# Which weight chunks are multiplied unsplit in fp32 behind four normalizations

## The reference, cut to what matters

```python
h = rms_norm(x, g_pre_mix)                    # norm 0
proj = h @ w_in                               # 1024 x 2560
...                                           # attention, recurrence
x = x + rms_norm(mix, g_post_mix)
h = rms_norm(x, g_pre_ffn)                    # norm 1
up = causal_dwconv(h @ w_up, w_conv_ffn)      # 1024 x 5632
x = x + rms_norm(ffn, g_post_ffn)
...
h = _rmsnorm(x) * (1 + scale) + shift         # norm 2, then norm 3
qkv = h @ w_qkv                               # 1024 x 3072
gate, up = jnp.split(h @ w_gu, 2, axis=-1)    # 1024 x 5632
```

## Time and profile before

| | |
|---|---|
| median of 3 runs | 1262.53 us (1262.05 to 1265.84) |
| span of the profiled execution | 1258.0 us |
| own time of that execution | not listed beside its span; the median of the runs is 4.5 us over the span |
| TensorE busy | 1224.1 us, 97% |
| VectorE busy | 1016.2 us, 81% |
| ScalarE busy | 779.0 us, 62% |
| GpSimd busy | 93.1 us, 7% |

### The profile page before, as it was taken

The page is one execution under the profiler, slowest core; times in us unless marked ns, Lnnn a source line. Parts: engine busy times, 40 slices in busy tenths (PEclk is TensorE's granted clock), DMA queues, the critical chain, the costliest instruction groups (busy, mean ns, idle before and its releaser), DMA issues.

```text
span 1258.0 us, 20244 instructions
## 1 busy us (share of the span) xinstructions
PE 1224.1 (97%) x7668; PEld 1086.8 (86%) x7668; DVE 1016.2 (81%) x1095; ACT 779.0 (62%) x992; POOL 93.1 (7%) x111
## 2 busy tenths in 40 slices
PE   9989999999999999999999999999999999999995
PEld 7978999987998799998897777898989898989884
DVE  6797899996756588777756578989898989898987
ACT  5765666644655455443346556777777777777764
POOL 0020000000562100000002202000000000000020
PEclk9999999999999999999999999999999999999998
DMA  9953997679944569998973239999999999999991
GB/s 322 377 200 102 337 314 270 246 289 252 250 159 162 181 215 325 332 349 308 382 253 97 79 140 394 379 406 355 401 351 409 348 408 349 408 345 411 347 410 73
DMA packets 163981, 369.08 MB, mean 293 GB/s; under 512 B 24420, under 2 KB 96559, under 8 KB 157511
## 3 DMA queue, kind: packets, MB, share of 16 engines
q1 hardware_dynamic: 157345, 350.72, 78.0%
q10 hardware_dynamic: 5094, 12.11, 2.5%
q0 software_dynamic: 1472, 5.28, 1.1%
HBM read 360.72 MB, written 14.70 MB: 298 GB/s over the span
## 4 chain that ended last, share of the span: by engine, by line
PE 71%; DVE 12%; ACT 4%; issue 4%; DMA 3%; SPq 3%; POOL 2%; ACTq 0%; DVEq 0%
PE ps L1341 20%; PE ps L795 7%; PE ps L797 7%; PE ps L796 7%; PE ps L1368 6%; PE ps L807 4%; PE ps L809 4%; PE ps L811 4%; DVE wlo L1893 3%; SPq L712 2%; PE ps L859 2%; PE ps L867 2%; DMA raw<-in_moe_w_gu 2%; DVE third_lo L1893 2%; DVE wlo L1885 1%
## 5 line engine op out<-in xcount | busy, mean ns | idle before, releaser
L1406 ACT ACTIVATE whi<-raw 128x1024 fp32r<-128x1024 f32 x186 | 192.6, 1057 | 152.0 <-PE ps L797 96.1
L1885 DVE TENSOR_TENSOR wlo<-raw,whi 128x1024 fp32r<-128x1024 f32 x186 | 227.1, 1248 | 72.8 <-ACT whi L1406 69.3
L795 PE MATMUL ps<-ahi,whi 128*128 128x256 f32 x832 | 234.3, 282 | 0.3 <-ACT qT L1591 0.3
L796 PE MATMUL ps<-alo,whi 128*128 128x256 f32 x832 | 231.8, 279 | 0.0
L797 PE MATMUL ps<-ahi,wlo 128*128 128x256 f32 x832 | 231.8, 279 | 0.0
L1893 DVE TENSOR_TENSOR wlo<-raw,whi 128x1792 fp32r<-128x1792 f32 (+1 forms) x96 | 199.3, 2089 | 24.4 <-ACT whi L1420 24.3
L1420 ACT ACTIVATE whi<-raw 128x1792 fp32r<-128x1792 f32 (+1 forms) x96 | 167.5, 1758 | 55.9 <-PE ps L1368 24.0
L795 PEld LDWEIGHTS ps<-ahi,whi 128*128 128x128 f32 x832 | 156.9, 189 | 1.7 <-issue 0.8
L796 PEld LDWEIGHTS ps<-alo,whi 128*128 128x128 f32 x832 | 156.7, 188 | 0.7 <-issue 0.7
L797 PEld LDWEIGHTS ps<-ahi,wlo 128*128 128x128 f32 x832 | 156.9, 189 | 0.0
L1341 PE MATMUL ps<-whi,hchi 128*128 128x448 f32 x352 | 101.8, 370 | 4.0 <-DVE wlo L1893 2.7
(11 more groups left out here) (350 smaller groups left out, 2431.7 us busy)
## 6 DMA issues: line engine op xcount, KB each, us to landing
raw<-in_moe_w_gu SPq DMA_DIRECT2D x96, 896.0 KB, 7.0
ada<-in_w_ada SPq DMA_DIRECT2D x48, 1024.0 KB, 7.4
raw<-in_moe_w_down SPq DMA_DIRECT2D x32, 1024.0 KB, 7.9
ada<-in_moe_w_gu SPq DMA_DIRECT2D x32, 896.0 KB, 7.3
raw<-in_w_up SPq DMA_DIRECT2D x22, 1024.0 KB, 5.8
raw<-in_ffn_w_gu SPq DMA_DIRECT2D x22, 1024.0 KB, 9.1
ada<-in_moe_w_down SPq DMA_DIRECT2D x16, 1024.0 KB, 9.2
raw<-in_na_w_qkv SPq DMA_DIRECT2D x12, 1024.0 KB, 8.4
```

Of the source, the lines that this page charges most:

```text
L795: pe.matmul(o, h[:, k, cols], bhi[:, k], start=(k == 0), stop=False)
L796: pe.matmul(o, h[:, k, cols], blo[:, k], start=False, stop=False)
L1406: act.activation(high_, src, ACT.Copy).then_inc(hi_done, 1)
L1885: ve.tensor_tensor(low_, src, high_.bitcast(F32), ALU.subtract).then_inc(lo_done, 1)
```

## The change

Behind norms 0 to 3 only the first weight chunk stays unsplit. The second is split like all others, and its two ScalarE copies and two VectorE subtractions are put into the norm itself: ScalarE copies both halves right behind the last square root, before it modulates tile 1 (at norm 0, behind the activation copies). VectorE subtracts the first half before the four `alo`, the second half behind them (at norm 0, both behind them). TensorE's order at norms 1 to 3 becomes: turn tile 0; tile 0 of the first chunk, its first column tile and then its second; turn tile 1; tile 1 of the first chunk; the second chunk in split form. `gate_up` starts at its first step and leaves out its first chunk, and `projection` starts with chunk 1; the wait for the activations' pairs moves from the third chunk to the second. Since the second chunk now fills a split buffer, the fourth chunk's copies wait for it. `whole_pair` stays in use for the latent attention (norm 4), whose chunks are both unsplit as before.

```diff
+SECOND_CHUNK = {0: W_IN + 1, 1: W_UP + 1, 2: W_QKV + 1, 3: W_GU + 1}
-WHOLE = [c for first in (W_IN, W_UP, W_QKV, W_GU, W_MDN) for c in (first, first + 1)]
+WHOLE = [W_IN, W_UP, W_QKV, W_GU, W_MDN, W_MDN + 1]
...
-            def whole_columns(first, s, banks, after_turn=None):
-
-                pieces = two_tiles(banks)
-                w = whole_pair(first, s, (256, 256), pieces, after_turn)
-                for i in range(2):
-                    whole_rest(w[i], pieces[i], s)
+            def whole_columns(first, s, bank, after_turn=None):
+
+                fill(2, {1: 0, 3: 2}.get(s, 0))
+                turn(s, 0)
+                if after_turn:
+                    after_turn()
+                w = whole_raw(first, 256)
+                pieces = two_tiles((bank,))[0]
+                for piece in pieces:
+                    whole_side([(w, piece)], 0, s)
+                turn(s, 1)
+                whole_rest(w, pieces, s)
...
             def gate_up(gu, stage):
-                for j in range(1, GU_STEPS):
+                for j in range(GU_STEPS):
...
-                        columns_form(gu + 2 * j + part, [ps[:, 2 * (j % 2) + part, f * S:(f + 1) * S] for f in range(2)], ahi, alo,
-                                     AT0[stage] if (j, part) == (1, 0) else None)
+                        if (j, part) != (0, 0):
+                            columns_form(gu + 2 * j + part, [ps[:, 2 * (j % 2) + part, f * S:(f + 1) * S] for f in range(2)],
+                                         ahi, alo, AT0[stage] if (j, part) == (0, 1) else None)
...
-            for c in range(2):
-                if c:
-                    pe.wait_ge(sem("vecs_ready"), 1)
-                w = whole_raw(W_IN + c, 256)
-                for piece in first_pair[c]:
-                    whole_side([(w, piece)], 0, 0)
-                whole_rest(w, first_pair[c], 0)
+            w0 = whole_raw(W_IN, 256)
+            for piece in first_pair[0]:
+                whole_side([(w0, piece)], 0, 0)
+            whole_rest(w0, first_pair[0], 0)
+            pe.wait_ge(sem("vecs_ready"), 1)
+            columns_form(W_IN + 1, [o for o, _ in first_pair[1]], ahi, alo, AT0[0])
...
-            for c in range(2, 12):
-                pe.wait_ge(sem("qkv2_free"), c - 1)
+            for c in range(1, 12):
+                if c >= 2:
+                    pe.wait_ge(sem("qkv2_free"), c - 1)
...
+                if s in SECOND_CHUNK and s:
+                    split(SECOND_CHUNK[s])
                 modulate_tile(s, 1, scale, shift)
...
             norm_by_tile(0, vec("g_pre_mix"))
+            split(W_IN + 1)
...
+                if s:
+                    split(SECOND_CHUNK[s], (0,))
                 for n in range(KT // 2):
...
+                split(SECOND_CHUNK[s], (1,) if s else (0, 1))
```

More of the change, by code:

```diff
@@ L870, in whole_pair @@
             def whole_pair(first, s, widths, pieces, after_turn=None, before_turn=None):
-                fill(2, {1: 0, 3: 2}.get(s, 0))
                 turn(s, 0)
@@ L1080, in projection @@
             def projection(first, c, rows, b, free, stage, step):
-                turn0 = AT0[stage] if c == 2 else None
+                turn0 = AT0[stage] if (stage, c) == (2, 1) else None
                 if rows:
@@ L1126, in _ @@
             sum_columns(0, (0,), 3)
-            whole_columns(W_UP, 1, (0, 1), lambda: sum_columns(0, (1,), 3, KT))
+            whole_columns(W_UP, 1, 0, lambda: sum_columns(0, (1,), 3, KT))
             pe.wait_ge(sem("mod_read0"), 1)
@@ L1130, in _ @@
             output_projection(W_DOWN, FT, tiles(ghi), tiles(glo), 1, sem("gT_ready1"))
-            whole_columns(W_QKV, 2, (6, 7))
+            whole_columns(W_QKV, 2, 6)
             def step2(i):
@@ L1159, in _ @@
             output_projection(W_NAO, KT, *mixes[2], 2, begun=2, last=HEADS0[3] // 2)
-            whole_columns(W_GU, 3, (0, 1))
+            whole_columns(W_GU, 3, 0)
             gate_up(W_GU, 3)
```

## The result

Twelve executions of each kernel on the same chip: before 1261.20 us median, after 1266.39. The ratio is 1.0038, 95% interval 1.0025 to 1.0052, so the change costs 0.4%, some 4.8 us (the medians are 5.2 apart), just beyond the 0.3% that the prediction gave as what a measurement of this kernel can tell. One execution of the kernel before took 4995.69 us; it hardly moves the median. The forecast was no change, 1262.5 us in a range to 1266.2; the median lies just above that range, and the change made the kernel slower. The forecast's starting point, 1262.53 us from three executions, was itself 1.3 us above the median of the twelve.

The account below looks back on a forecast made before the run. The prediction took TensorE's order of work as the bound (busy 1224 of 1258 us). Its terms, -1.5 - 1.5 + 3.9 - 0.9, summed to 0.0 us, so 1262.5 us, range 1258.0 to 1266.2.

Parts of the forecast that it names:

- norm 0: Norm 0: chunk 1's halves come in time and the attention behind passes the saving on; -1.5 us, bounds 0 to -1.5.
- norm 1: Norm 1: the saving is kept, with under 0.1 us of modulation showing; 10.72 us becomes 9.23, so -1.5.
- norm 2, order and meeting: Norm 2: lost cover and VectorE meeting GpSimd's additions outweigh the saving; +3.9 us, bounds -1.2 and +3.9.
- norm 3: Norm 3: the order costs 0.2 us at the turn and 0.15 at the modulation; -0.9 us net, bounds -0.5 and -1.5.
- (a): Norm 2, tile 0: the whole second column tile follows the wait, so tile 1's turn and everything behind come 0.8 us later.
- (b): Norm 2: VectorE's subtractions alternate with GpSimd's bias additions, which start at 319.73 whatever TensorE does; 1.06 us lost each time.
- (c): Norm 2: TensorE waits for VectorE in the second chunk; the third chunk starts at 331.8 instead of 327.88, so +3.9 us.
- the bias for the second eight heads: Norm 2: its additions cost GpSimd another 11.01 us later, independently of TensorE, and could give back 0.3 us.
- the doubt in that step: Norm 0: unknown whether attention, paced by VectorE and queued transfers until 60 us, passes the gain on: 0 to -1.5 us.
- Rival D: Slower, by the clock: norm 2's waits bring low-clock stretches of 1.7 us; one gives 1264.2, two 1265.9, three 1267.6; chance 0.14.
- that place as safe: Norm 2, 309.5 to 313.3 us: TensorE busy 2.08 of 3.80 us, yet the clock kept 1.00.
- the common term: All four edits: an unsplit chunk takes 7.15 us, a split one 5.63; each saves 1.5 us of TensorE work, 6.1 in all.

Follow-up runs that it names:

- the changed kernel again: The changed kernel, unaltered, run a second time with a new profile: 1.0034 (1.0015 to 1.0052) of the kernel before.
- the pair without the additions: Changed kernel and kernel before, each without GpSimd's first eight mask additions at norm 2: 0.9955 and 1.0000 of the kernel before; medians 1258.74 and 1262.94 us.
- the later start: GpSimd's first eight mask additions at norm 2 wait for third-chunk splits: changed kernel 1.0004, kernel before 0.9986, norms 0 to 2 0.9992, norms 0 and 1 0.9983.
- the kernel before again: The kernel before, unaltered, run again with a new profile: 1.0000; the profiled execution took 1263.20 us.

## Why the prediction was wrong

From turn to turn, all profiles (20 in all; at norm 2 those with GpSimd's additions left out or moved are left out, and at norm 1 the one with small matmuls):

| term | forecast | measured | from |
|---|---|---|---|
| norm 0 | -1.5 | -0.5 | 107.5 (mean of 11) against 108.0 (9) |
| norm 1 | -1.5 | -1.11 | 190.33 to 190.37 against 191.44 to 191.48 |
| norm 2, order and meeting | +3.9 | +4.0 | 137.86 (one profile) against 133.9 (mean of 7), no low clock in any |
| norm 2, low clock in tile 0 and a fifth meeting | 0 | +0.8 | mean of 6 is 138.64, the one with dummy matmuls among them; +0.5 if the old order's one profile with a low clock is counted too (134.1, mean of 8) |
| norm 3 | -0.9 | -0.6 to -0.8 | 196.03 against 196.59, 191.55 against 192.32 |
| sum | 0.0 | +2.6 | |
| share of the long pitch behind norm 3 | not in it | +2.1, an estimate | norm 3 alone is +1.3 to +1.6, less its own -0.6; each of the two is uncertain by 2 |

The last two lines together are +4.7 us; the three comparisons of the changed kernel with the kernel before gave +4.8, +4.3 and +5.2. The same terms give +4.8 for norm 2 alone (measured +4.8), +3.2 for norms 0 to 2 (+3.2), -0.1 for norms 0, 1 and 3 (+0.1), -1.1 for norm 1 (-1.8) and -1.6 for norms 0 and 1 (+0.3, in the interval). These agreements bear out the sum and not each term: every measured value is uncertain by some 2 us.

**Norm 2** was right in mechanism and in size, by its three steps. (a) The turn of tile 1 comes 7.86 us behind that of tile 0, 6.97 before: 0.89 for 0.8. (b) 1.07 us a meeting for 1.06. The count was short: GpSimd did not start at 319.73 "whatever TensorE does" but at 316.69, 10.2 us behind the turn and not 11.2 (in the profiles with its additions in their place it started anywhere from 9.2 to 13.3 us behind), and all four activation subtractions met it. With the earliest start seen under the new order, 9.5 us in the changed kernel again, the first added subtraction met it too (2.1 us), the fifth meeting of the table. TensorE was 2.05 us earlier itself, so only 1 us of the 3 counted. (c) The third chunk came 24.6 us behind the turn in place of the forecast 23.3, and attention took some of it back, so that +4.0 meets +3.9 as closely as it does is in part luck. The Trainium skill ("SBUF — State Buffer", SBUF: two separate sides) says that GpSimd and a VectorE operation with two SBUF inputs take the shared ports by an exclusive lock, each for a whole instruction. The trace agrees: 0.63 us alone, 1.70 beside GpSimd, the same loss for every one. What I added at the end of that part, that the bias for the second eight heads could give something back, did not matter.

**Norm 1** lost 0.39 us of its 1.5 where I had said that under 0.1 would show: the matmuls of tile 1 start 1.04 us behind the turn's start in place of 0.87 and take 3.94 us, not 3.74, which I put down to the modulation that nothing covers now. **Norm 3** loses the same way: tile 1 takes 4.13 us for 3.74. **Norm 0** is a step that failed: I gave its bounds as 0 and -1.5 and took the full end. The raw saving came as forecast: from the first turn to the recurrence's gates, the first matmuls behind the projection, TensorE takes 29.03 us before and 27.53 in the one changed profile with the same pitch there. But by the turn of norm 1 only 0.5 of it is left in the mean. In the two first profiles the lead is still 2.2 us at the last scores before 65 us; then TensorE stands 2.41 us instead of 1.55 for the attention's `probs`, and the lead is 1.0 by 83 us. So the attention between took it back, as the doubt in that step said; which engine or transfer paces it was not tested. These three are 1.6 us of the miss.

**The clock.** Rival D had the right sign. At norm 2 the nine profiles with the new order have twelve low stretches of 3.4 us (one of 6.8 counted as two), the other eleven have one. But the price is by place. Behind the stops of the second chunk a stretch cost nothing in the first profile, since the third chunk waits for VectorE anyway (137.85 us with one, 137.86 without). In tile 0, at 311 us, it costs 1.1 to 1.5 (turn to turn of the tiles 8.9 to 9.4 us against 7.86; 10.07 with the one of 6.8 us). The Trainium skill ("TensorE: Matmul & The Clock Gate", HAM oscillation) describes the like, short bursts of matmuls with waits between them behind which the clock is low; the trace agrees here in six of nine profiles. I had read that place as safe because the clock kept 1.00 there in the earlier trace rows. With the new order the first gap there is as before (1.10 us), the burst behind it is shorter (8 matmuls in 1.44 us instead of 16 in 2.02) and the second gap longer (1.22 us instead of 0.64). The stretch at 64 to 66 us costs nothing that shows: 107.06 to 107.94 us with it, 107.38 and 107.91 without. Nine of the eleven profiles with the new norm 0 have it and one of the nine others. D's price for a stretch, 1.7 us, was too high, and where it asked for three, or for two with norm 0's gain lost, there were one or two at norm 2 and two thirds of norm 0's gain was lost. With 0.5 to 0.8 us in the mean the clock is the smaller part of the miss.

**The pitch** is the step that failed by omission, and the largest single term of the miss as far as it can be estimated. In the common term I noted two paces, 0.117 and 0.113 us, and took them for a property of the stage, the same before and after. They are two paces of one stream: behind norm 3 the kernel before has either, 4.3 us apart. The changed norm 3 has the long one in eight of nine profiles, the old one in five of eleven, and one of 23 executions against 24 of 51 was in the lower group. That is supported by counts and not shown, and the pair without the additions speaks against it. Behind norm 0 the traces show the same two paces in a run of 96 split matmuls, and there the edit goes with the short one: 113.3 ns in ten of eleven profiles with the new norm 0, in two of nine with the old. Nine microseconds of that run, before and after:

```profile
27.00:36.00 9.00, 9.00 (x78) 9.00 (x78) 6.96 (x13) 4.47 (x5) 0.00 (x0) 1.00 1.05 372
26.00:35.00 9.00, 9.00 (x82) 9.00 (x81) 6.35 (x14) 7.83 (x12) 0.00 (x0) 1.00 1.05 380
```

That is worth 0.4 us at 36 us, and part of the 0.5 us that norm 0 gave: at the short pitch the stage ahead of norm 1 takes 107.6 us with the old order (two profiles) and 107.5 with the new (ten), at the long one 108.1 (seven) and 107.5 (one). How the start of a stream selects the pitch is not shown. The long streams behind norms 1 and 3 all begin with the same instructions, the first split matmul 28 to 29 ns behind its weight load. Whether the one or two unsplit chunks ahead of it, the waits in them, or something outside the kernel decides was not separated. That something outside has a part is likely: in one group of runs none of 29 executions of the kernel before was below 1261 us, in another 25 of 31 were. The two were on different chips; on the chip of the 25 of 31, a later group had 14 of 29.

## What to carry to other kernels

Before a VectorE instruction with two SBUF inputs is moved to a place, look for what GpSimd does there and when it starts: each meeting cost a fixed time here (1.07 us, whether the subtraction alone takes 0.63 or 1.18), and what GpSimd does may be easier to move than what VectorE does. Then look at what stands behind it in GpSimd's own list: the later start gave back 2.6 us through it. A gain on the bound engine counts only from turn to turn: the stage behind has to be checked for an engine that takes it back. And when the same group of matmuls shows two paces in one trace, ask for a second trace of the same program before either enters a sum.

## What the runs showed of the hardware

A stream of 960 or 1008 matmuls of 128x256, each with its own weight load, ran at 113.3 or at 117.8 ns a piece at the same granted clock (1.00), and kept what it had from its first few matmuls to its end. Behind norm 1 it was 117.8 in all 20 profiles, behind norm 3 either, and so was a run of 96 of them behind norm 0. TensorE counts as fully busy in both, so only the number of instructions in a window tells them apart.

Four neighbours 499 us into two executions, timeline of TensorE (start, us, what). The kernel before with the additions moved has the short pitch, the kernel before again the long one:

```profile
498.76 0.28 PE L795 MATMUL ps<-ahi,whi 128*128 128x256 f32 x1
498.87 0.28 PE L796 MATMUL ps<-alo,whi 128*128 128x256 f32 x1
498.98 0.28 PE L797 MATMUL ps<-ahi,wlo 128*128 128x256 f32 x1
499.10 0.28 PE L795 MATMUL ps<-ahi,whi 128*128 128x256 f32 x1
```

```profile
498.89 0.28 PE L795 MATMUL ps<-ahi,whi 128*128 128x256 f32 x1
499.00 0.28 PE L796 MATMUL ps<-alo,whi 128*128 128x256 f32 x1
499.12 0.28 PE L797 MATMUL ps<-ahi,wlo 128*128 128x256 f32 x1
499.24 0.28 PE L795 MATMUL ps<-ahi,whi 128*128 128x256 f32 x1
```

A two-column fp32 matmul put into such a stream cost 0.22 us (4.4 us for 20 of them), about twice the time of a 256-column one.
